# Sums of the last down weights moved from the last block product into the rounds of the second FFN of a Hymba layer, with the order around both changed

## The reference

```python
def swiglu(x, w_gate, w_up, w_down):
    return (jax.nn.silu(x @ w_gate) * (x @ w_up)) @ w_down

h = swiglu(rmsnorm(x, ffn1_pre_norm[i]), ffn1_w_gate[i], ffn1_w_up[i], ffn1_w_down[i])
x = x + MACARON_WEIGHT * rmsnorm(h, ffn1_post_norm[i])
h = hybrid_mixer(rmsnorm(x, mix_pre_norm[i]), ...)
x = x + rmsnorm(h, mix_post_norm[i])
h = swiglu(rmsnorm(x, ffn2_pre_norm[i]), ffn2_w_gate[i], ffn2_w_up[i], ffn2_w_down[i])
x = x + MACARON_WEIGHT * rmsnorm(h, ffn2_post_norm[i])
```

## Time and profile before

| | us |
|---|---|
| median of 3 runs | 2276.1 |
| lowest and highest run | 2273.67 to 2276.16 |
| the profiled execution, its own time | 2276.56 |
| its span in the profile | 2274.8 |
| TensorE busy | 2209.6 (97%) |
| VectorE busy | 1741.1 (77%) |
| ScalarE busy | 965.1 (42%) |
| GpSimd busy | 350.4 (15%) |

### The profile page before, as it was taken

How to read it: one execution, slowest core, us unless ns; L and a number is a source line. 1 busy time by engine, 2 the same in 40 slices (tenths; PEclk the granted TensorE clock), 3 DMA queues, 4 the chain that set the end, 5 groups by cost and what they waited for, 6 DMA issues and landing times.

```text
span 2274.8 us, 29629 instructions
## 1 busy us (share of the span) xinstructions
PE 2209.6 (97%) x10304; PEld 1809.2 (80%) x10304; DVE 1741.1 (77%) x2550; ACT 965.1 (42%) x1725; POOL 350.4 (15%) x290
## 2 busy tenths in 40 slices
PE   9999999999999999999999999999899999989989
PEld 7888888888877877778788777788788888868867
DVE  8877777777759777786666676878877777789997
ACT  6322222222334576787531674224422323335443
POOL 0000000000000344444100225100000000033572
PEclk9999999999999999999999999999999999999999
DMA  4111111111323001001121234132122222285734
GB/s 161 54 53 43 54 55 55 55 40 47 117 98 125 20 10 38 29 18 57 59 82 47 75 119 174 60 100 105 53 87 83 83 83 83 83 312 201 231 116 148
DMA packets 78179, 199.83 MB, mean 88 GB/s; under 512 B 8448, under 2 KB 10496, under 8 KB 76288
## 3 DMA queue, kind: packets, MB, share of 16 engines
q1 hardware_dynamic: 78080, 198.56, 26.0%
HBM read 165.69 MB, written 32.83 MB: 87 GB/s over the span
## 4 chain that ended last, share of the span: by engine, by line
PE 84%; DVE 7%; ACT 3%; issue 3%; POOL 2%; DMA 1%; SPq 0%; DVEq 0%; ACTq 0%; POOLq 0%
PE psum L473 11%; PE psum L474 11%; PE psum L475 11%; PE psum L641 4%; PE psum L643 4%; PE psum L642 4%; PE psum L2437 3%; PE psum L2439 3%; PE psum L2438 3%; PE psum L1517 3%; PE psum L1519 3%; PE psum L1518 3%; PE psum L2583 2%; PE psum L2980 1%; PE psum L2594 1%
## 5 line engine op out<-in xcount | busy, mean ns | idle before, releaser
L1476 POOL TENSOR_TENSOR down_w_raw<-down_w_raw,down_w_two 128x512 f32<-128x512 f32 x55 | 88.0, 1611 | 665.0 <-DMA down_w_two<-in_d 664.9
L770 ACT CAST t_hi<-t_raw 128x512 fp32r<-128x512 f32 x152 | 93.6, 621 | 204.4 <-DVE t_raw L991 151.3
L1190 DVE TENSOR_TENSOR acc<-psum,acc 128x512 f32<-128x512 f32 x144 | 98.9, 691 | 80.5 <-PE psum L643 79.1
L792 ACT ACTIVATE sum<-sum 128x512 f32<-128x512 f32 x76 | 48.1, 633 | 231.7 <-DVE sum L1130 139.7
L1517 PE MATMUL psum<-down_b_hi,down_w_hi 128*128 128x512 f32 x308 | 123.0, 400 | 8.9 <-DVE down_w_lo L1508 8.9
L2437 PE MATMUL psum<-norm_hi,tile_hi 128*128 128x512 f32 x320 | 129.1, 403 | 1.9 <-DVE z_scaled L2845 1.9
L2754 DVE TENSOR_TENSOR probs_t_lo<-psum,probs_t_hi 128x512 fp32r<-128x512 f32 x144 | 97.1, 685 | 39.8 <-ACT probs_t_hi L2671 38.9
L473 PE MATMUL psum<-norm_hi,plain_hi 128*128 128x512 f32 x304 | 119.2, 392 | 7.5 <-DVE up_lo L1013 7.5
L2439 PE MATMUL psum<-norm_hi,tile_lo 128*128 128x512 f32 x320 | 125.0, 391 | 0.0
L2438 PE MATMUL psum<-norm_lo,tile_hi 128*128 128x512 f32 x320 | 124.8, 390 | 0.0
L766 ACT CAST plain_hi<-up_raw 128x512 fp32r<-128x512 f32 x76 | 47.1, 619 | 180.7 <-DMA up_raw<-in_gu 177.9
(11 more groups left out here) (456 smaller groups left out, 6477.9 us busy)
## 6 DMA issues: line engine op xcount, KB each, us to landing
down_w_raw<-in_d SPq DMA_DIRECT2D x77, 256.0 KB, 2.9
gate_raw<-in_gu SPq DMA_DIRECT2D x38, 512.0 KB, 4.3
up_raw<-in_gu SPq DMA_DIRECT2D x76, 256.0 KB, 3.9
raw_tile<-in_w_att SPq DMA_DIRECT2D x28, 512.0 KB, 3.6
down_w_two<-in_d SPq DMA_DIRECT2D x55, 256.0 KB, 4.4
act_scratch<-act_stage SPq DMA_DIRECT2D x21, 512.0 KB, 5.2
tile_lo_raw<-in_d SPq DMA_DIRECT2D x20, 512.0 KB, 4.2
x_scratch<-acc SPq DMA_DIRECT2D x32, 256.0 KB, 2.0
```

The costliest lines, as they stand in the source:

```text
L770: act.copy(to, of).then_inc(sem(p + "_t_hi"), 1)
L1190: v.tensor_tensor(x, banks(4 + d % 4), x, ALU.add).then_inc(sem(p + "_acc"), 1)
```

## The change

Four things.

1. The weight sums are made during the rounds. For each row tile k SP loads the two tiles of down weights (512 KB each) into `w_sum_in`; GpSimd makes all five sums of them in four steps, one of 128x1024 and three of 128x512 (`w_sum_pool`), into `w_sum_out`; SP stores them, 1.31 MB, to a DRAM tensor `down_w_sums`. In the last block product one load of 256 KB per (m, k) fetches a finished sum. SP's loop over pairs is written out; with n = 2(i-1)+s, the loads for k stand behind the last `v_next` of the tile n = 3k//2, and the store one tile later, ahead of the loads of the next k where both fall into one tile. So loads are issued at n = 0, 4, 6, 10, 12 (s = 0) and at n = 1, 3, 7, 9, 13, 15 (s = 1).
2. All activation sums are VectorE's. GpSimd does nothing in the last block product.
3. The difference has a buffer of its own, `x_difference_turn`, and waits for the second token half of the input alone; the turn's ranks put the sums, casts and low parts of the first seven-product tile (`t_sum`, `t_hi`, `t_lo`) to the front.
4. The last product, m = 6, goes through k with all four banks; the step `last` is gone, and what waited for it waits for the last row tile.

```diff
-DOWN_W = (((1, 0), (1, 1), ALU.add), ((0, 0), (1, 1), ALU.add), ((1, 1),), ((0, 1), (1, 1), ALU.subtract),
-          ((0, 0), (0, 1), ALU.add), ((0, 0),), ((1, 0), (0, 0), ALU.subtract))
+DOWN_W = {2: (1, 1), 5: (0, 0)}
+W_SUM = {4: 0, 0: 1, 1: 2, 3: 3, 6: 4}
-POOL_B = (5, 6)
...
+        d3_turn = at("x_difference_turn", 164, [P, KH, HALF])
...
+                for n in range(2 * LAST_PAIR - 1):
+                    i, s = 1 + n // 2, n % 2
+                    g_next(i, s)
+                    v_next(i, s, 0)
+                    if n:
+                        store(1 + (n - 1) // 2, (n - 1) % 2)
+                    else:
+                        wait(sp, p + "_prod", 4)
+                        for m in range(2):
+                            sp.dma_start(acts[m], stage[m][:]).then_inc(sem("act_out"), 16)
+                    v_next(i, s, 1)
+                    if n == 0:
+                        sp.wait_ge(sem("half_out"), 16 * past_half("t3", 0, KT))
+                        wait(sp, p + "_s_dve", 13)
+                    for k in range(FG):
+                        if 3 * k // 2 == n:
+                            w_sum_in(sp, k)
+                        if 3 * k // 2 + 1 == n:
+                            w_sum_out(sp, k)
...
+        def w_sum_in(sp, k):
+            wait(sp, "dn_ws_sum", 4 * (k - 1))
+            for n in range(2):
+                sp.dma_start(ws_in[k % 2][:, n], a["d2"][FG * n + k]).then_inc(sem(f"dn_ws_in{k % 2}"), 16)
+
+        def w_sum_pool(g, k):
+            (left, right), to = (ws_in[k % 2][:, n] for n in range(2)), ws_out[k % 2]
+            wait(g, f"dn_ws_in{k % 2}", 32 * (k // 2 + 1))
+            wait(g, f"dn_ws_out{k % 2}", 16 * (k // 2))
+            g.tensor_tensor(to[:, 0:2].rearrange("p a o c -> p (a o) c"), left, right, ALU.add).then_inc(sem("dn_ws_sum"), 1)
+            g.tensor_tensor(to[:, 2], left[:, 0:4], right[:, 4:8], ALU.add).then_inc(sem("dn_ws_sum"), 1)
+            g.tensor_tensor(to[:, 3], right[:, 0:4], right[:, 4:8], ALU.subtract).then_inc(sem("dn_ws_sum"), 1)
+            g.tensor_tensor(to[:, 4], left[:, 4:8], left[:, 0:4], ALU.subtract).then_inc(sem("dn_ws_sum"), 1)
+
+        def w_sum_out(sp, k):
+            wait(sp, "dn_ws_sum", 4 * k + 4)
+            sp.dma_start(wsum[k], ws_out[k % 2][:]).then_inc(sem(f"dn_ws_out{k % 2}"), 16)
...
         def down_start_sp(sp, store):
             sp.wait_ge(sem("act_out"), 16 * 2 * LAST_PAIR)
+            for n in range(2):
+                wait(sp, f"dn_ws_out{n}", 16 * ((FG + 1 - n) // 2))
             down_w_in(sp, 0, 0)
             down_w_in(sp, 0, 1)
-            sp.wait_ge(sem("half_out"), 16 * past_half("t3", 0, KT))
-            wait(sp, "f2_s_dve", 21)
...
         def down_product_pe(pe, m, k):
-            last = m == DOWN_N - 1
-            if k == FG:
-                down_bank_free(pe, m, 3)
-                for n in range(FG):
-                    mm = down_three(pe, m, n, 3)
-                mm.then_inc(sem("dn_mm"), 1)
-                return
             wait(pe, "dn_w_lo", FG * m + k + 1)
             wait(pe, "dn_b_lo", FG * m + k + 1)
-            for d in range(3 if last else 4):
+            for d in range(4):
```

More of the change, by code:

```diff
@@ L742, in difference_hi @@
                     wait(act, p + "_gu_mm", 3)
-                act.activation(nh[:, k, half(0)], d3[:, k, :], ACT.Copy, scale=gain(k)).then_inc(sem(p + "_s_act"), 1)
+                act.activation(nh[:, k, half(0)], (d3 if t == "t0" else d3_turn)[:, k, :], ACT.Copy, scale=gain(k)).then_inc(sem(p + "_s_act"), 1)
             def s4_copy(n):
@@ L801, in tile @@
                     wait(act, p + "_read", at_tile(i, s, 11, 8 - 11))
+                    if isinstance(i, int) and i == 1 and not s:
+                        wait(act, p + "_prod", 4)
                     act.copy(e1[:], banks(0)).then_inc(sem(p + "_s_out"), 1)
@@ L1391, in build @@
         GROUPS_OF_ROWS = ((0, 4), (4, 8), (8, FG))
-        def w_loads(m):
-            return sum(min(len(x), 2) for x in DOWN_W[:m + 1])
-        def w_sums(m, k):
-            return FG * sum(len(x) > 1 for x in DOWN_W[:m]) + k + 1
         def b_sums(m, k):
-            same = [n for n in range(m) if len(DOWN_B[n]) > 1 and (n in POOL_B) == (m in POOL_B)]
-            return FG * len(same) + k + 1
+            return FG * sum(len(x) > 1 for x in DOWN_B[:m]) + k + 1
+        def w_sum_in(sp, k):
[13 more added lines that the diff above has]
+            sp.dma_start(wsum[k], ws_out[k % 2][:]).then_inc(sem(f"dn_ws_out{k % 2}"), 16)
         def puts_to(m, d):
@@ L1415, in down_b_summed @@
         def down_b_summed(eng, m, k):
-            wait(eng, "dn_b_sum_pool" if m in POOL_B else "dn_b_sum", b_sums(m, k))
+            wait(eng, "dn_b_sum", b_sums(m, k))
         def down_slot(eng, m, k):
@@ L1439, in down_w_in @@
                 wait(sp, "f2_read", at_tile(LAST_PAIR, 1, 11, 11))
-            for n, (out, rows) in enumerate(DOWN_W[m][:2]):
-                to = dw_two[k] if n else dw_raw[k]
-                sp.dma_start(to[:], a["d2"][FG * rows + k][:, 4 * out:4 * out + 4]).then_inc(sem(f"dn_w_in{k}"), 16)
+            if m in W_SUM:
+                of = wsum[k][:, W_SUM[m]]
+            else:
+                out, rows = DOWN_W[m]
+                of = a["d2"][FG * rows + k][:, 4 * out:4 * out + 4]
+            sp.dma_start(dw_raw[k][:], of).then_inc(sem(f"dn_w_in{k}"), 16)
         def down_rows_in(sp, rows, h, g, name):
@@ L1598, in end_plan @@
                         if len(DOWN_B[m]) > 1:
-                            in_pool = m in POOL_B
-                            add("POOL" if in_pool else "DVE", "b_sum", ("b_sum", m, k), 1.45 if in_pool else 0.69, free)
+                            add("DVE", "b_sum", ("b_sum", m, k), 0.69, free)
                             b = ("b_sum", m, k)
@@ L1608, in end_plan @@
                             ready.append(("rb", "t3_post0"))
-                    add("PE", "main", ("mm", m, k), 2.04 if m == DOWN_N - 1 else 2.72, *ready)
-                if m == DOWN_N - 1:
-                    add("PE", "main", ("last",), 7.5)
+                    add("PE", "main", ("mm", m, k), 2.72, *ready)
                 for d in range(4):
-                    done = ("last",) if (m, d) == (DOWN_N - 1, 3) else ("mm", m, FG - 1)
+                    done = ("mm", m, FG - 1)
                     users = put_in(m, d)
@@ L1965, in turn_plan @@
             sums += [(0.69, [("resid", "t2", 1, KH + k)]) for k in range(KH)]
-            sums += [(2.2, [("round", 2, KT - 1)])] + [(0.69, [("difference_hi", k)]) for k in range(KH)]
+            sums += [(2.2, [("resid", "t2", 1, KT - 1)])] + [(0.69, [("difference_hi", k)]) for k in range(KH)]
             sums += [(2.3, [("sum_copy", 1)]), (2.3, [("sum_copy", 0)])] + [(1.22, [("s4_copy", n)]) for n in range(2)]
@@ L1972, in turn_plan @@
             for k in range(KH):
-                add("ACT", "s", ("difference_hi", k), 0.63, ("planned_sum", 12))
+                add("ACT", "s", ("difference_hi", k), 0.63, ("planned_sum", 12), ("round", 0, KT - 1))
             for n in range(2):
@@ L3355, in _ @@
             for step, *e in END["PE"]:
-                if step in ("mm", "last"):
-                    down_product_pe(pe, *(e or (DOWN_N - 1, FG)))
+                if step == "mm":
+                    down_product_pe(pe, *e)
                 elif step in LATE_STEPS:
@@ L3438, in _ @@
             gate_pool(g)
-            for k in range(EARLY):
-                down_w_sum(g, 0, k)
-            for step, *e in END["POOL"]:
-                if step == "w_sum":
-                    down_w_sum(g, *e)
-                else:
-                    down_b_sum(g, *e)
+            for k in range(FG):
+                w_sum_pool(g, k)
 def shape_constants():
```

67 lines of the change are left out of this document (19 added, 48 removed).

## The result

The changed kernel takes 2315.76 us (median of 4 runs, 2310.62 to 2316.74) where the kernel before takes 2276.13. The ratio is 1.0171, 95% interval 1.0154 to 1.0189: slower by some 40 us. The prediction was 2304.1 us with a range of 2267 to 2320.

A forecast was written before the change was run, and what follows sets the result against it. TensorE, busy 2209.6 of 2274.8 us, was taken as the bound, any new wait paid in full. The terms -6.5 + 36 - 2.8 + 0.3 + 1.0 gave +28.0, a span of 2302.8 and median of 2304.1 us, range 2267 to 2320.

The forecast's parts named there:

- The turn, A: Before the first seven-product tile: the earlier low part cuts TensorE's wait and slow clock, -6.5 us (-5.0 to -7.3).
- The rounds, B: Rounds: eleven sets of GpSimd weight sums hold VectorE and make TensorE wait, +36 us (0 to 61.6).
- the reserve of a quarter microsecond: Rounds, second tiles: the add that frees the last product's bank can slip only 0.26 us before TensorE waits.
- the 0.83 I took: Turn, used for the rounds: 0.83 us from a VectorE step's start to the matmul that it releases.
- while TensorE is slow VectorE catches up: Rounds: most slow clock behind long waits is not paid twice, so only 1.6 us was added.
- The signs: Rounds: waits of 3 to 5 us before first to fourth products in six tiles, 1 to 2 in others, some 34 in all.
- The start of the last block product, C: Start of the last block product: summed weights arrive in one load and VectorE's steps shorten, -2.8 us (0 to -5).
- ScalarE now casts all weights ahead of b_hi_3: Start of the last block product: a brake named against 4.4 us from shorter VectorE steps, within a forecast of -2.8.
- The join, D: Between sixth and seventh product: late square sums, columns, rows and slow clock cost 14.8 us, +0.3 (-4 to +2).
- The end, E: Behind the last matmul: four banks' adds and square sums remain where one bank's did, +1.0 us (0 to 2).
- the sums are free: Rounds: GpSimd's sums fit in VectorE's pauses and cost 0, giving 2268 us; chance 0.15.
- The whole step holds: Rounds: GpSimd holds VectorE for whole steps, 1.29 and 2.41 us, costing 45 with low clock, giving 2313; chance 0.10.

The follow-up runs named there:

- measured -6.1 alone: Kernel before with only the turn's part: the difference in its own buffer and the new ranks; 2270.27 us against 2276.35 in the runs beside it.
- the casts in pairs: Changed kernel with GpSimd's sets in VectorE's pauses, plus ScalarE's first-product casts as weights k, activations k instead of all weights first; 2264.33 us.
- the experiment: Changed kernel with the seventh product as in the kernel before, three banks by row tiles, then the fourth; 2313.27 us.
- the placing in the pauses: Changed kernel, but GpSimd starts each set only after VectorE's last low part for the next tile, nine sets in first tiles; 2273.71 us.

## Why the prediction was right, and where its sizes were off

The direction, the large term and its mechanism held, and the sum was 12.1 us too low (a span of 2302.8 forecast, 2314.9 measured). By the starts of the matmuls the five terms measured -6.1, +43.6, -0.8, +1.9 and +1.5, where -6.5, +36, -2.8, +0.3 and +1.0 were forecast; all five missed to the same side.

*The turn, A.* Forecast -6.5 (-5.0 to -7.3), measured -6.1 alone. The wait fell from 7.45 to 2.64 us where I said some 2. The rounds begin 7.0 us earlier in the changed kernel and their first tile is 0.9 longer at slow clock (22.03 and 21.09 us). One detail was wrong: what releases TensorE is no longer the low part (L1013, now L1017, which started at 1633.42) but the up rescale, L2087.

```profile
1635.36 0.79 PE L472 MATMUL psum<-norm_hi,plain_hi 128*128 128x512 f32 x1 [2.64 <-DVE up_scaled L2087]
```

*The rounds, B.* Forecast +36, measured +44.5, or 43.6 without the 0.9 of the first tile. The mechanism is the one worked out: two-input steps hold each other at a rhythm of 1.70 us, the delay of the last low part passes through the gate load to the add that frees the bank, the reserve of a quarter microsecond is nothing, and first tiles are cheaper than second ones. The 1.1 us for a GpSimd step of 512 columns were met (1683.06, 1684.77, 1686.46). At each such wait the matmul follows the add's start by 0.73 or 0.74 us, less than the 0.83 I took, so the reserve was some 0.35 us and not 0.26. The term that was mis-sized is the six sets of second tiles, by what a wait brings with it: 36.4 us, where 26.4 and a part of the 1.6 were forecast, though their listed waits are only 24.9. The five sets of first tiles were forecast at 8.0 and cost 7.1. I forecast 34.4 us of waits and 1.6 of slow clock, "while TensorE is slow VectorE catches up". The trace lists 17 waits in the rounds, 29.7 us. By the starts of the matmuls the stops cost 37.3: each has about 0.3 us of edges that are in no wait (the matmul ahead of it is shown 0.39 long where its share is 0.23, and the one behind starts its successor 0.33 later), and there are some more stops too short to be listed. Matmuls at half clock cost 7.2 us more than before. 37.3 + 7.2 = 44.5. The windows behind the wait of 4.96 us:

```profile
1696.00:1698.00 2.00, 0.00 (x0) 0.00 (x0) 2.00 (x4) 0.68 (x2) 0.00 (x0) 0.53 1.00 421
1698.00:1700.00 2.00, 1.61 (x4) 1.32 (x5) 1.87 (x4) 0.90 (x2) 0.00 (x0) 0.50 0.30 128
1700.00:1702.00 2.00, 2.00 (x7) 1.52 (x6) 1.87 (x4) 0.84 (x2) 0.00 (x0) 0.50 0.00 0
1702.00:1704.00 2.00, 2.00 (x8) 1.63 (x7) 1.97 (x4) 0.62 (x1) 0.00 (x0) 0.76 0.02 4
```

TensorE runs at half clock for over 4 us behind it, some 2 us lost, and that three times. Nothing of it comes back: the tile behind each lasts 19.05 to 19.07 us. The signs were partly elsewhere than I said: the three long waits stand before a tile's last product, not its first to fourth, and in the first tiles the fourth product waited for ScalarE's copy `first_product`, not for the low part from which I took the room.

*The start of the last block product, C.* Forecast -2.8. The wait is 9.4 us where it was 8.9 in four pieces; with edges and slow clock the product loses 12.0 us where it lost 12.8, so 0.8 was gained. The step that failed: "ScalarE now casts all weights ahead of b_hi_3" stood in my text as a small brake, with the gain read from VectorE's shorter steps. It was the whole wait, as the casts in pairs show: with them the loss is 0.3.

*The join, D.* Forecast +0.3: 12.3 us from the last matmul of the sixth product to the seventh, and 2.5 of slow clock. Measured: 8.05 us to the columns, then

```profile
2265.65 2.08 PE L1678 MATMUL psum<-square_sums,ones 128*128 128x512 f32 x2 [1.29 <-DVE square_sums L1673]
2268.49 0.77 PE L1526 MATMUL psum<-down_b_hi,down_w_hi 128*128 128x512 f32 x1 [0.77 <-ACT rstd_rows L1682]
```

14.0 us from 2254.47 to 2268.49. It is 1.7 us more than my 12.3: 0.8 for the square sum and 0.9 for the rows, which take 2.08 where the earlier trace rows have 1.23. They ran at a granted clock of 0.50 throughout, those before at a mean of 0.69 (2222.90 to 2223.60). The slow clock behind costs 2.2, near the 2.5. In all the join loses 16.4 us where it lost 14.5.

*The end, E.* Forecast +1.0, measured +1.5 behind the last matmul (14.5 us to the end of the span where it was 13.0). The 2.05 of the experiment are the whole rest of that kernel.

C, D and E together were to give -1.5 and gave +2.6. So of the 12.1 us between forecast and result 7.6 are B's, by what comes with the waits, 2.0 are C's, 1.6 D's, 0.5 E's and 0.4 the turn's.

The rival "the sums are free" is what the placing in the pauses made true. "The whole step holds" was near the time (2313) for a wrong reason: a 512-column step held VectorE for 1.1 us and not 1.29, the large one for 1.85 to 2.2 and not 2.41, and the listed waits, 29.7 us, were below the 34.4 forecast.

## What to carry to other kernels

Work that is moved to an idle engine is free only if it doesn't share a path with a busy one: look not at the share of busy time but at the stretch where the work will land, and start it there by a count that the busy engine gives (here one wait on GpSimd and the choice of the tiles were worth 42 us, 2273.71 against 2315.76). A wait on a full engine must be priced with its edges and the slow clock behind it: 29.7 us of listed waits were 44.5 us here. And when a list of one engine holds steps that wait for a late load, put nothing behind them that is needed sooner.
